# Weighted sum by pairs of slots, a ring of ten row buffers, and a router that holds half the heads

## The reference, cut to what matters

```python
qd = (xb @ w_query).reshape(-1, PEER_HEADS, 2, PEER_DQ // 2)
s1, s2 = scores of the two halves of qd against sub_keys1, sub_keys2
v1, i1 = top_k(s1, 16); v2, i2 = top_k(s2, 16)
top_s, pos = top_k(v1[..., :, None] + v2[..., None, :], 16)
idx = take_along_axis(i1 * 128 + i2, pos)
g = softmax(top_s)
u = expert_down[idx]
act = gelu(einsum('thkd,td->thk', u, xb), approximate=False)
out = einsum('thk,thkd->td', g * act, expert_up[idx])
```

## Time and profile before

| | |
|---|---|
| median of three runs | 4535.72 us |
| the profiled execution's own time | 4559.18 us |
| its span, first to last instruction | 4557.7 us |
| first gather issued, last dot of the tiles begun | 1438.4 us, 4505.4 us |
| dots (L1890), 1024 of | 1226 ns each, 1249.1 us |
| gather issues (L1781), 1024 of | 1117 ns each, 1143.5 us |
| matmul instructions of the sum (L1818), 4096 of | 1022 ns each, 894.2 us busy |
| mean granted TensorE clock | 0.728 of full speed |

### The profile page before, as it was taken

The page is one execution under the profiler, slowest core; times in us unless marked ns, Lnnn a source line. Parts: engine busy times, 40 slices in busy tenths (PEclk is TensorE's granted clock), DMA queues, the critical chain, the costliest instruction groups (busy, mean ns, idle before and its releaser), DMA issues.

```text
span 4557.7 us, 41634 instructions
## 1 busy us (share of the span) xinstructions
PE 2459.0 (54%) x12785; PEld 1314.5 (29%) x12785; DVE 2349.4 (52%) x4723; ACT 969.8 (21%) x3037; POOL 1294.8 (28%) x1232
## 2 busy tenths in 40 slices
PE   7799995679994533543353353344335325334433
PEld 1697773245543300210120031022013002102200
DVE  0651103556645665466356446646645654663564
ACT  1110112134431221222212221221222222222122
POOL 0120111300001433333333333333333333433332
PEclk9799996789996766765675576566567557656666
DMA  7232212453226999999999999999999999999997
GB/s 262 74 101 104 96 44 75 182 179 100 88 68 263 366 363 351 373 361 370 341 365 359 349 367 363 359 351 366 361 352 362 371 348 363 364 363 361 367 362 273
DMA packets 216787, 1286.18 MB, mean 282 GB/s; under 512 B 27923, under 2 KB 53147, under 8 KB 80204
## 3 DMA queue, kind: packets, MB, share of 16 engines
q0 software_dynamic: 159504, 1114.68, 63.8%
q1 hardware_dynamic: 57046, 168.82, 10.9%
HBM read 1235.04 MB, written 48.36 MB: 282 GB/s over the span
## 4 chain that ended last, share of the span: by engine, by line
DMA 34%; issue 13%; PE 10%; POOL 6%; ACT 5%; DVE 1%; POOLq 0%; ACTq 0%; DVEq 0%; SPq 0%
DMA e_buf<-in_experts,e_idx 33%; PE ps L1818 10%; POOL e_buf L1781 6%; ACT e_wts L1862 2%; ACT e_diag L1866 2%; DVE e_buf L1890 1%; ACT e_acts L1860 1%; PE ps L1524 1%; DMA e_buf<-in_experts,e_idxT 0%; POOLq L59 0%; DMA r_wq<-in_w_query 0%; ACTq L1865 0%; POOLq L60 0%; PE ps L1838 0%; DVE r_pos L1583 0%
## 5 line engine op out<-in xcount | busy, mean ns | idle before, releaser
L1890 DVE SCALAR_TENSOR_TENSOR e_buf<-e_buf,e_h 128x1024 f32<-128x1024 f32 x1024 | 1249.1, 1226 | 1295.4 <-DMA e_buf<-in_experts,e_idx 1240.0
L1818 PE MATMUL ps<-e_buf,e_diag 128*32 128x512 f32 x4096 | 894.2, 1022 | 1824.9 <-ACT e_diag L1866 1824.9
L1781 POOL DMA_INDIRECT e_buf<-in_experts,e_idx x1024 | 1143.5, 1117 | 1818.0 <-PE ps L1818 1562.1
L1818 PEld LDWEIGHTS ps<-e_buf,e_diag 128*32 128x32 f32 x4096 | 149.5, 155 | 2370.9 <-ACT e_diag L1866 2048.2
L1860 ACT ACTIVATE e_acts<-e_dots 128x4 f32<-128x4 f32 x256 | 52.6, 205 | 2321.8 <-DVE e_buf L1890 2321.8
L1524 PEld LDWEIGHTS ps<-r_h2T,r_wq 128*128 128x128 f32 x2304 | 290.6, 209 | 101.5 <-issue 101.4
L1524 PE MATMUL ps<-r_h2T,r_wq 128*128 128x128 f32 x2304 | 303.2, 294 | 3.1 <-DMA r_wq<-in_w_query 3.1
L1866 ACT ACTIVATE e_diag<-e_eye,e_wts 128x32 f32<-128x32 f32 x1024 | 245.8, 310 | 25.9
L835 PE MATMUL ps<-xo_w_out,xo_catT 128*128 128x512 f32 x512 | 224.6, 592 | 1.7 <-DVE xo_x L868 1.7
L1862 ACT ACTIVATE e_wts<-e_acts,e_gate 128x1 f32<-128x1 f32 x1024 | 217.6, 282 | 8.3
L75 PE MATMUL ps<-p_wth,hT_high 128*128 128x512 f32 (+1 forms) x432 | 170.6, 395 | 10.9 <-PEq L418 10.9
(11 more groups left out here) (343 smaller groups left out, 3058.7 us busy)
## 6 DMA issues: line engine op xcount, KB each, us to landing
w_mod_sb<-in_w_mod SPq DMA_DIRECT2D x12, 2048.0 KB, 8.1
e_h<-h_d SPq DMA_DIRECT2D x128, 128.0 KB, 11.5
e_buf<-in_experts,e_idx POOLq DMA_INDIRECT x1024, 9.2
p_wt<-in_w_rows SPq DMA_DIRECT2D x6, 2048.0 KB
proj_d<-p_ev POOLq DMA_DIRECT2D x48, 256.0 KB, 2.3
x_zgv<-proj_d SPq DMA_DIRECT2D x8, 1536.0 KB, 6.4
p_w<-in_w_chan SPq DMA_DIRECT2D x20, 512.0 KB, 4.3
r_wq<-in_w_query SPq DMA_DIRECT2D x4, 2048.0 KB, 20.0
```

Of the source, the lines that this page charges most:

```text
L1781: return pool.indirect_dma_start(out=buf[s][:], out_offset=None, in_=io["experts"], in_offset=bass.IndirectOffsetOnAxis(ap=numbers, axis=0 ...
L1818: last = nc.tensor.matmul(out, diag[:, s, :], buf[s][:, D + cols * 512:D + (cols + 1) * 512], start=(q == 0), stop=(q == NG - 1))
L1890: V.scalar_tensor_tensor(out=down, in0=down, scalar=1.0, in1=row, op0=ALU.mult, op1=ALU.mult, accum_out=out).then_inc(sem, 1)
```

## The change

The ring has ten buffers in place of eight (RING = 10). Since 128 isn't a multiple of ten, `uses`, `landed_by` and `free_at` work out the counts that the waits ask for; buffers 8 and 9 are used 12 times in a tile and the others 13 times. ACT and PE work through a group as two pairs (PAIR = 2): one Gelu, two gate products and two diagonals for each pair, and eight matmul instructions that wait for that pair alone. The router's buffers hold four heads, so ACT copies the scores of the second half only when the first half's expert numbers are chosen, and the pieces have a new order and new tables. `f_gate`, `f_final` and `f_y` share one buffer `par`: the gate and the final weights are loaded again for every tile, SP does the store within `Finish.store` and waits for it before it loads `x1` and the gate, and the scaling moves from the eighth slot to the twentieth.

```diff
-RING = 8
+RING = 10
+PAIR = 2
...
+        def uses(k):
+            return -(-(SLOTS - k % RING) // RING)
+        def landed_by(n, k):
+            return n * (16 * uses(k)) + 16 * (k // RING) + 16
+        def free_at(n, k):
+            before = k - RING if k >= RING else k % RING + RING * (uses(k) - 1) - SLOTS
+            return n * SLOTS + before + 1 + RING
...
                 for k in range(SLOTS):
-                    wait_apart(pool, summed, n * SLOTS + k + 1)
+                    wait_apart(pool, summed, free_at(n, k))
                     if k in (0, HALF_SLOTS - RING):
...
-                    pe.wait_ge(weighed, n * SLOTS + (q + 1) * GROUP)
-                    for cols in range(2):
-                        for j in range(GROUP):
-                            s = (q * GROUP + j) % RING
+                    for pair in range(0, GROUP, PAIR):
+                        k0 = q * GROUP + pair
+                        pe.wait_ge(weighed, n * SLOTS + k0 + PAIR)
+                        for cols in range(2):
+                            for k in range(k0, k0 + PAIR):
+                                s, j = k % RING, k % GROUP
...
-                    act.wait_ge(dotted, n * SLOTS + (q + 1) * GROUP)
-                    ch.step(A(acts[:, ks], dots[:, ks], ACT.Gelu))
+                    for k0 in range(q * GROUP, (q + 1) * GROUP, PAIR):
+                        ks = slice(k0, k0 + PAIR)
+                        act.wait_ge(dotted, n * SLOTS + k0 + PAIR)
+                        ch.step(A(acts[:, ks], dots[:, ks], ACT.Gelu))
...
 (Router.tensor)
-            if b:
-                scores(b - 1)
+                if m == 1 and b % 2:
+                    scores(b - 1)
+                    yield
+            if b % 2:
+                scores(b)
                 yield
-        scores(3)
 (Router.scalar)
+            if b == 0 and routed:
+                act.wait_ge(self.chosen, n * 4)
+            scores(b)
...
+        act.wait_ge(self.chosen, n * 4 + 2)
+        for b in (2, 3):
+            scores(b)
...
 (Finish)
+    def load_gate(self, sp, x1, gate2, rs):
+        sp.dma_start(self.x1[0:rs, :], x1).then_inc(self.x1_in, 16)
+        sp.dma_start(self.par[0:rs, :], gate2).then_inc(self.gate_in, 16)
+    def store(self, sp, n, y, rs):
+        sp.wait_ge(self.r_ready, n + 1)
+        sp.dma_start(self.par[0:rs, :], self.g.io["norm_final"].partition_broadcast(rs)).then_inc(self.final_in, 16)
+        sp.wait_ge(self.y_ready, n + 1)
+        sp.dma_start(y, self.x1[0:rs, :]).then_inc(self.stored, 16)
+        sp.wait_ge(self.stored, n * 16 + 16)
...
-PE_PIECES = {q: 1 for q in (*range(1, 14), 18, 20, 27, 29)}
+PE_PIECES = {q: 1 for q in (*range(13), 15, 18, 27, 29)}
-ACT_PIECES = {q: 1 for q in (2, 4, 6, 7, 9, 10, 12, 13, 14, 18, 21, 26, 30)}
+ACT_PIECES = {1: 1, 3: 1, 5: 1, 6: 1, 7: 1, 9: 1, 12: 1, 15: 1, 16: 2, 19: 1, 27: 1, 30: 1}
-DVE_PIECES = {8: 2, 9: 3, 11: 2, 12: 3, 13: 2, 14: 2, 15: 2, 16: 2, 17: 4, 19: 1, 20: 4, 21: 3, 22: 3, 23: 3,
-              24: 3, 25: 4, 26: 3, 27: 1, 29: 1}
+DVE_PIECES = {6: 3, 7: 2, 8: 3, 9: 2, 10: 3, 11: 3, 12: 3, 13: 2, 14: 1, 17: 1, 18: 3, 19: 3, 20: 3, 21: 2, 22: 3,
+              23: 3, 24: 3, 25: 2, 26: 1, 28: 1, 30: 1}
...
-                    if k == 2 * GROUP - 1 and not first:
+                    if k == 5 * GROUP - 1 and not first:
                         fin.scale(dve, n - 1, P)
```

More of the change, by code:

```diff
@@ L1460, in __init__ @@
         self.h2 = sb("h2", [P, D])
[L1461 to L1468, removed]
+        H = PH // 2
+        self.h2T, self.qT = sb("h2T", [P, KD, P]), sb("qT", [P, PH, P])
+        self.work = sb("work", [P, PH, P])
+        self.v, self.iu, self.inum = sb("v", [P, PH, TOPK]), sb("iu", [P, PH, TOPK], U32), sb("inum", [P, PH, TOPK])
+        self.top, self.pos = sb("top", [P, H, TOPK]), sb("pos", [P, H, TOPK], U32)
+        self.part = sb("part", [P, 2, H, TOPK], U32)
+        self.row = sb("row", [P, 2, H, TOPK])
+        self.total, self.e = sb("total", [P, H]), sb("e", [P, H, TOPK])
         self.gate, self.num = sb("gate", [P, SLOTS]), sb("num", [P, SLOTS])
@@ L1548, in scalar, with queries @@
         yield
+        def queries(b):
+            act.wait_ge(self.q_ps, n * 4 + b + 1)
+            A(self.qT[:, b % 2 * 4:b % 2 * 4 + 4, :].rearrange("p k r -> p (k r)"), g.bank(4 + b),
+              ACT.Copy).then_inc(self.q_kept, 1)
         def scores(b):
             act.wait_ge(self.s_ps, n * 4 + b + 1)
[L1552 removed]
+            A(self.work[:, b % 2 * 4:b % 2 * 4 + 4, :].rearrange("p k r -> p (k r)"), g.bank(4 + b),
               ACT.Copy).then_inc(self.s_kept, 1)
[L1555 to L1557 removed]
+        for b in range(2):
+            queries(b)
             yield
[L1559 to L1563, removed]
+            if b == 0 and routed:
+                act.wait_ge(self.chosen, n * 4)
+            scores(b)
+            yield
+        for b in (2, 3):
+            queries(b)
+            yield
+        act.wait_ge(self.chosen, n * 4 + 2)
+        for b in (2, 3):
+            scores(b)
+            yield
         for half in range(2):
[L1565 removed]
             act.wait_ge(self.shifted, n * 2 + half + 1)
[L1567 removed]
+            A(self.e[:], self.e[:], ACT.Exp).then_inc(self.e_ready, 1)
             yield
@@ L1601, in vector @@
         pair = [P, H, TOPK, TOPK]
+        square = cand.rearrange("p h (a b) -> p h a b", b=TOPK)
         for half in range(2):
-            for b in (2 * half, 2 * half + 1):
-                wait_apart(dve, self.s_kept, n * 4 + b + 1)
+            for b in range(2):
+                wait_apart(dve, self.s_kept, n * 4 + 2 * half + b + 1)
                 yield from self.top16(ch, self.v, self.iu, lambda u: self.work[:, u, :], range(b * 4, b * 4 + 4))
[L1606 to L1611, removed]
+            ch.mark(V.tensor_copy(self.inum[:], self.iu[:]))
+            ch.step_apart(V.tensor_tensor(square, bcast(sides[:, :, 0, :].unsqueeze(3), pair),
+                                          bcast(sides[:, :, 1, :].unsqueeze(2), pair), ALU.add))
             yield
-            yield from self.top16(ch, self.top, self.pos, lambda h: cand[:, h, :], range(hs.start, hs.stop))
-            ch.mark(V.tensor_single_scalar(self.part[:, 0, hs], self.pos[:, hs], 4, ALU.logical_shift_right))
-            ch.step(V.tensor_single_scalar(self.part[:, 1, hs], self.pos[:, hs], TOPK - 1, ALU.bitwise_and))
+            yield from self.top16(ch, self.top, self.pos, lambda h: cand[:, h, :], range(H))
+            ch.mark(V.tensor_single_scalar(self.part[:, 0], self.pos[:], 4, ALU.logical_shift_right))
+            ch.step(V.tensor_single_scalar(self.part[:, 1], self.pos[:], TOPK - 1, ALU.bitwise_and))
             yield
@@ L1620, in vector @@
                 ch.step(V.tensor_tensor(hit, bcast(self.g.iota16[:].unsqueeze(1).unsqueeze(1), pair),
-                                        bcast(self.part[:, side, hs].unsqueeze(3), pair), ALU.is_equal))
+                                        bcast(self.part[:, side].unsqueeze(3), pair), ALU.is_equal))
                 yield
-                ch.step(V.tensor_tensor(hit, hit, bcast(numbers[:, hs, side, :].unsqueeze(2), pair), ALU.mult))
-                summed = V.tensor_reduce(self.row[:, side, hs], hit, AXX, ALU.add)
+                ch.step(V.tensor_tensor(hit, hit, bcast(numbers[:, :, side, :].unsqueeze(2), pair), ALU.mult))
+                summed = V.tensor_reduce(self.row[:, side], hit, AXX, ALU.add)
                 if side == 0:
@@ L1845, in _ @@
             A = nc.scalar.activation
-            own = rt.scalar(act, 0)
+            own = rt.scalar(act, 0, False)
             drive(own, 11)
```

126 lines of the change are left out of this document (55 added, 71 removed).

## The result

The changed kernel takes 4230.94 us, the median of four runs (4226.78 to 4232.68); the kernel before took 4538.18 beside it (4535.12 to 4550.28). The ratio is 0.9317, its 95% interval 0.9298 to 0.9336: 307 us less. The forecast was 4400, with 4320 as the lower end of its range. So the direction came true, and the gain is more than twice the one forecast.

The account below looks back on a forecast made before the run. DMA transfers were taken to bound the kernel, with a ring just too short. From the profiled 4559.2 us, -135 (tile middles), -5 (start) and +3.3 (end) gave 4422.5, scaled to the median 4400; range 4320 to 4500.

Parts of the forecast that it names:

- The bound, and the two parts: Gather stage: DMA transfers set the pace, an eight-buffer ring has 0.5 us reserve; ten buffers and pairs give 11 us.
- The full rate: Middle of a tile: runs full at 383 GB/s, 353.3 to 336.4 us, a gain of 135 us in eight tiles.
- the two small terms: Ends of the kernel: -5 us ahead of the first gather, +3.3 us at the last scaling.
- The turn with pairs: Gather ring: a buffer's turn falls from 21.4 to 15.0 us, 16.3 for a pair's second; ten buffers give 27.4.
- The change of tiles: Where one tile follows another: DMA already full, share 0.97 at 336 GB/s, so left unchanged.
- Loads, instructions, router: Each tile: repeated loads take 3.1 us, counted in the middle; 52 us of added Gelu hidden; router order costs nothing.
- Ahead of the first gather: Before the gathers: scores come earlier, 6 us off, first Exp waits some 1 us; -5 taken, between 0 and -6.
- The end: Last scaling waits for a load after the norm: +3.3 us, from 0 to +12 if the earlier store is late.
- A: Rival, middle of a tile: DMA has no reserve, stays at 363 GB/s, new loads paid in full; 4559 us, chance 0.09.
- B: Rival, TensorE: a pair's eight matmuls last as long as sixteen, 3.64 us; no change, 4535 us, chance 0.08.
- C: Rival, router pieces and a tile's end: reserve gone now and then, half the gain; 4467 us, chance 0.13.
- The signs named: Tile middles about 336 us, 380 GB/s or more, share 0.98; POOL's wait under 1562 us, VectorE's above 1000; first gather before 1438.

## Why the prediction was right, and where it went wrong

The forecast missed by one term of its sum, the rate of a full tile: 383 GB/s were taken, 414 to 421 came.

**The bound, and the two parts (right).** DMA transfers with a ring just too short: with neither part the kernel is the one before, with either it is at full rate, with six gathers out it is back. None of the rivals came true.

**The full rate (the step that failed).** "What is full? ... I take 383, since the longest stretch is nearest to a whole tile." The term assumes that a filled queue moves data as the fullest stretches of before did. It doesn't: the middles run at 414 or 415 GB/s, and at 421 in a stretch of 40 us. With 414 the same sum gives 128.85 / 0.414 = 311.2 us for a tile's middle in place of 336.4: 42.1 us a tile and 337 in eight. With the two small terms as measured (-7.4, +1.3) that is 4559.2 - 337 - 6 = 4216, against 4230.7 for the profiled execution after. What is left, 15 us, fits the change of tiles below.

Why was 383 wrong? The stretches of the earlier trace rows come from a kernel whose ring ran short every few gathers, and even the fullest of them held late landings. In the stretch at 383 most dots that wait for a gather start some 2.5 us apart, but these two start 4.04 and 3.49 us after the dot before:

```profile
1884.47 1.23 DVE L1890 SCALAR_TENSOR_TENSOR e_buf<-e_buf,e_h 128x1024 f32<-128x1024 f32 x1 [2.82 <-DMA e_buf<-in_experts,e_idx]
...
1895.52 1.23 DVE L1890 SCALAR_TENSOR_TENSOR e_buf<-e_buf,e_h 128x1024 f32<-128x1024 f32 x1 [2.25 <-DMA e_buf<-in_experts,e_idx]
```

The longest stretch was nearest to a whole tile in length, but not to a queue that never empties; the shortest, 400 over 20 us, was nearer. A row of the kernel before had it, and the prediction didn't read it: dots that each wait for a landing, in a run without a gap. From VectorE's timeline of before:

```profile
2691.65 1.23 DVE L1890 SCALAR_TENSOR_TENSOR e_buf<-e_buf,e_h 128x1024 f32<-128x1024 f32 x1 [1.23 <-DMA e_buf<-in_experts,e_idx]
...
2694.14 1.23 DVE L1890 SCALAR_TENSOR_TENSOR e_buf<-e_buf,e_h 128x1024 f32<-128x1024 f32 x1 [1.25 <-DMA e_buf<-in_experts,e_idx]
...
2696.62 1.22 DVE L1890 SCALAR_TENSOR_TENSOR e_buf<-e_buf,e_h 128x1024 f32<-128x1024 f32 x1 [1.25 <-DMA e_buf<-in_experts,e_idx]
```

Landings 2.49 us apart are 1.049 / 2.49 = 421 GB/s, the very rate of the full stretch after. (These rows are no exception: of 698 neighbouring dots of before that both wait for a landing, the median distance is 2.49 us.) With it the prediction's own turn would have read otherwise: 3 x 2.49 + 7.9 + (5.3 - 2.49) + 2.49 = 20.7 us, against 8 x 2.49 = 19.9 for eight buffers. The reserve wasn't 0.5 us but 0.8 us short: by this sum the ring falls short even without a delay. The sum doesn't give the pace, though: the turn measured was 22.9 us, 2.2 more.

The gain of a tile's middle, 353.3 to 311 us, has two halves. Filling the share from 0.947 to 1.00 gives some 19 us, near the 17 of the forecast. The other 23 come from packets that take less time; that half the prediction put at next to nothing, since it took a rate at which packets were still slow.

**The turn with pairs (right).** Forecast: sum and reissue 7.0 us, measured 7.06; turn 15.0 us, and 16.3 for the second of a pair. At 2.49 us a gather the same sum is 2.49 + 7.06 + 2.9 + 2.49 = 14.9, and 16.2 for the second. Six gathers out give 14.9, seven 17.4, eight 19.9: six too few, seven with 1.2 us in hand, eight with 3.7. The runs show the edge there: with six nothing is left of the gain, with seven 1.5% is missing, with eight nothing. The sum sorts the cases; it doesn't give the pace below the edge. At 369 GB/s six out turn in 6 x 2.84 = 17.0 us, not in 16.2.

**The change of tiles ("I leave as it is": wrong by a little).** It is worse, 297 GB/s in 30 us against 336: 39 x 30 / 1000 = 1.2 MB less, 2.8 us at 414 GB/s, 20 us in seven changes. VectorE now waits 67.5 us in 14 waits for the rows of `e_h`, where it waited 11.2 in 3. Two of them:

```profile
2465.33 1.23 DVE L1914 SCALAR_TENSOR_TENSOR e_buf<-e_buf,e_h 128x1024 f32<-128x1024 f32 x1 [4.98 <-DMA e_h<-h_d]
...
2471.09 1.23 DVE L1914 SCALAR_TENSOR_TENSOR e_buf<-e_buf,e_h 128x1024 f32<-128x1024 f32 x1 [4.52 <-DMA e_h<-h_d]
```

That 15 us were missing in the sum and that this stretch lost 20 is a match of sizes; the run with the rows ahead shows that moving these loads doesn't win the time back, and the runs with copied rows win some 7 us a tile of it by the loads' form.

**Loads, instructions, router (right).** The two loads were put at 3.1 us a tile; the run without one of them gives 1.2 to 1.8 for that one. ScalarE's 256 more Gelu are hidden: 25% busy. SP still has time to spare, 2615 us in its three longest waits:

```profile
SPq L1781 <- DVE e_buf L1914: 1939.6, 28, 352.0
SPq L1681 <- ACT f_r L1707: 416.6, 9, 211.5
SPq L1683 <- DVE f_x L1698: 258.9, 9, 35.5
```

The transposes of `r_h` at group 0 wait for nothing, as forecast: issued at 2451.73, read at 2476.95, right behind the group's matmuls.

```profile
2451.73 0.35 SPq L1784 DMA_DIRECT2D r_h<-h_d  x1
...
2473.60 3.42 PE L1841 MATMUL ps<-e_buf,e_diag 128*32 128x512 f32 x16 [18.92 <-ACT e_diag L1890]
...
2476.95 1.10 PE L1506 MATMUL ps<-ident,r_h 128*128 128x128 f32 x8
```

**Ahead of the first gather: -5, measured -7.4. The end: +3.3, measured +1.3.** From the last tile's last dot to the end pass 53.6 us in place of 52.3. Both waits that the prediction named are there. The earlier store's scaling waits 12.77 us, but the last eight gathers go on meanwhile; the last one waits 6.21, against 4.34.

```profile
4195.99 1.28 DVE L1698 SCALAR_TENSOR_TENSOR f_x<-f_x,f_r,f_par 128x1024 f32<-128x1024 f32 x1 [12.77 <-DMA f_par<-in_norm_final]
...
4224.60 1.27 DVE L1698 SCALAR_TENSOR_TENSOR f_x<-f_x,f_r,f_par 8x1024 f32<-8x1024 f32 x1 [6.21 <-DMA f_par<-in_norm_final]
```

**The rivals.** *A* (the missing 5% are gaps that no buffer closes) fell: share 1.00. The Trainium skill, DMA: Bandwidth & Descriptors (Where 436 GB/s comes from), says that some 358 GB/s of HBM bind such loads; 421 over 40 us, here on one core, don't agree. The Trainium skill, Perfetto Trace Analysis (Roofline), takes about 120% of 358, some 430, as the practical ceiling of a single active core; 421 is 118%, and that does agree.

*B* (a pair's eight matmuls last as long as sixteen) had its premise right, 3.63 us against 3.64 at the same granted clock, and its conclusion wrong. A pair's gathers take 2 x 2.49 = 4.98 us, more than the 3.63, and the granted clock of the middles rose from 0.65 to 0.79 or more, nearer to 2.4 GHz, and at 0.86 a pair took 2.18 us. TensorE waits 1103.3 us for the diagonals:

```profile
PE ps L1841 <- ACT e_diag L1890: 1103.3, 414, 19.7
```

*C* (half the gain) fell too: the middles hold no dips.

**The signs named.** A share of 0.98 or more, POOL's wait shorter and not gone (1221.8), the earlier first gather: as forecast. VectorE's wait for gathers "still above 1000" is 864.5, and the middles are shorter than 336. The second follows from the rate; the first would too (1024 gathers, each 0.25 us shorter than at 383 GB/s, are 256 us), but no run parts it.

## What to carry to other kernels

Where a ring just fails to cover its turn, the fullest stretches of its trace can still understate the transfer rate, as here; read the rate from landings that follow one another while a consumer waits for each, and work out the turn with that. Then any one way of keeping enough transfers out is worth the whole gain, and a second is worth nothing; here, with pairs, eight gathers of 1 MB were enough and seven nearly, while with groups of four eight were too few and ten enough. Once the queue is full, every byte and the form of every load counts: here rows brought by sixteen loads of 32 partitions cost three times as much a byte as the gathers.

## What the runs showed of the hardware

With pairs, the same 159504 gather packets took 2935 us of DMA time with six gathers out, 2775 with seven and 2745 to 2750 with eight or ten: busy DMA engines weren't equally productive, so a share of 0.95 hid more than 5%, 353 us a tile's middle against 311. Loads of 32 partitions, sixteen for 2.1 MB, cost 7 us a MB where gathers cost 2.4; the same rows in four loads of 128 partitions cost 6 / 2.1 = 2.9. The change of tiles shows a share of 1.02 at 297 GB/s, that is, DMA engines counted as busy that moved little. The granted clock of the middles rose from 0.65 to 0.80, with TensorE busy 63% of them in place of 43%, and the time didn't depend on it: ten buffers without pairs kept 0.66 and the whole gain.
